# Attention by pairs of heads, run three chunks behind the query projection

## The chip, the cores and the metric

The kernel runs on one NeuronCore of a Trainium2 chip. A core has a tensor engine (PE, with its weight loads PEld), a vector engine (DVE), a scalar engine (ACT), GpSimd (POOL) and a sync engine (SP), which here issues the loads of weights. The metric is device time in microseconds (us), the median of three runs. The kernel before takes 1352.44 us (1351.33 to 1356.03).

## The reference

One inference step of a two-layer encoder with width 1024: layer 0 is RWKV-7 time mixing and a mixture of experts, layer 1 is window attention and a mixture of experts. There are 256 prompt frames and 64 sample frames, so 320 in all, in five chunks of 64. The change touches only the attention of layer 1:

```python
def sink_probs(s, sink, mask):
    ...
    m = jnp.maximum(jnp.max(s, axis=-1, keepdims=True), sink)
    e = jnp.exp(s - m)
    return e / (jnp.sum(e, axis=-1, keepdims=True) + jnp.exp(sink - m))

# 16 query heads, 4 key/value heads, head size 64; a chunk of 64 queries sees its own
# chunk of keys and the two before (the sample chunk: 128 cached keys and its own 64)
    q = (h @ p['at_w_q'][j] + p['at_b_q'][j]).reshape(B, S, N_HEADS, HEAD_DIM)
    q = rope_partial(q, pos)
    s = jnp.einsum('bnqkgd,bnskd->bnkgqs', qc, kb).astype(jnp.float32) * ATT_SCALE
    ...
    o = jnp.einsum('bnkgqs,bnskd->bnqkgd', probs.astype(vb.dtype), vb)
    return o @ p['at_w_o'][j] + p['at_b_o'][j]
```

## The kernel before

Activations lie transposed: 1024 features as eight blocks `c` of 128 partitions, 320 time columns each. A block of the queries `q[:, c, :]` holds two heads of 64 rows, called a pair below; pairs 2g and 2g+1 share key/value head g. All of it is in float32.

Each engine runs its own list of instructions in program order. A key such as `("prob", n, c)` stands for a count of finished instructions on one engine; `wait` on it holds everything behind it on the waiting engine. PSUM has eight banks, taken in turn by `Banks.open`, which waits until the bank's last reader is done.

After the experts of layer 0, PE makes the key and value projections, turns the values into rows of tokens (`v64`), and then makes the query projection: for every block c, eight matmuls of 128x320 (`project`), and, one block late, a matmul with the rotation matrix (`q_turn`). ACT adds the bias while it copies out of PSUM; DVE applies cosine and sine (three operations a block).

Then comes the attention proper, by time chunks n = 0 to 4, each over all 16 heads at once. `scores(n)` writes four banks of 16 heads x 64 queries x W keys, W being 64, 128, 192, 192, 192. DVE takes the row maxima and combines them with the sinks (`row_maxima`), ACT takes exponentials with row sums (`exps`, one instruction for a pair, then one for the sinks), DVE adds, inverts and scales (eight instructions). PE turns the probabilities in pieces of 64 keys (`attended`, line 1181), ACT copies these out of PSUM, and PE multiplies them with the values. On PE the order is: scores(0), scores(1), attended(0), scores(2), attended(1), and so on: the scores of chunk n+1 stand between those of chunk n and the turning of chunk n's probabilities. The output projection (`project("ao", ...)`) waits for the whole of it. SP loads the second half of its weights when the query projection has released the slot, and the first experts' weights of layer 1 behind it in the same queue.

Of the kernel before, what the change touches and what calls it, by code (L numbers as in the profile page):

```python
# [237 lines left out]
def build(nc, i, o, known, seen):  # L238
    ctx = ExitStack()
    with ctx:  # L240
# [22 lines left out]
        sink = sb("sink", [P, C])  # L263
        att2 = sb("att", [P, 2, 6, C])
# [98 lines left out]
        hkv, haq, q, qt, oT = E[1], E[5], E[6], E[7], E[5]  # L363
# [6 lines left out]
        v64 = work[0:64, 4 * B:4 * B + 7 * 256].rearrange("p (n d) -> p n d", n=7)  # L370
        k64 = work[0:64, 4 * B + 1792:4 * B + 2560].rearrange("p (n d) -> p n d", n=3)
        prob2 = [work[:, a:a + 1536].rearrange("p (c s) -> p c s", c=C) for a in (0, 7 * B)]
        pT = work[0:64, 1536:1536 + 3072].rearrange("p (w c s) -> p w c s", w=3, c=C)
# [212 lines left out]
        def _(eng):  # L586
# [65 lines left out]
            eng.dma_start(v64[:, 4:6, :], i["cache_v"][0].rearrange("(w t) n d -> t w (n d)", w=2)  # L652
# [5 lines left out]
            pl.wait("v64")  # L658
            for n_out, w, t0 in ((5, 2, 0), (5, 3, 64), (9, 6, 0)):
                put(o[n_out][0, t0:t0 + 64].rearrange("t n d -> t (n d)"), v64[:, w, :])  # L660
# [12 lines left out]
        def _(eng):  # L673
# [460 lines left out]
            for w, t0 in enumerate((0, 64, 128, 192, 256)):  # L1134
                pb = bank.open("v64", w)
                for c in range(2):
                    ins = eng.transpose(pb[0:64, P * c:P * c + P], vT[:, c, t0:t0 + 64], ident)
                full(ins, "v64", w)
# [11 lines left out]
            for c in range(C):  # L1150
                project("q", [c], haq, lambda hf: ("wq", hf), ("h", "A1"))
                if c:
                    q_turn(c - 1)
            q_turn(C - 1)
            pe.wait("kswapped", 1)

            def scores(n):
                t0 = CH * n
                lo, hi = (max(0, n - 2) * CH, (n + 1) * CH) if n < 4 else (256, 448)
                for b in range(4):  # L1160
                    pe.wait("q ready", 2 * b + 1)
                    pb = bank.open("score", n, b)
                    for cc in range(2):
                        c = 2 * b + cc
                        g = c // 2
# [5 lines left out]
                    full(ins, "score", n, b)  # L1171

            def attended(n):
                prob = prob2[n % 2]
                parts = min(n + 1, 3) if n < 4 else 3
                for w in range(parts):
                    for hf in range(2):
                        pe.wait("prob", n, 4 * hf + 3)
                        pb = bank.open("pT", n, w, hf)
                        for cc in range(4):  # L1180
                            ins = eng.transpose(pb[0:64, P * cc:P * cc + P], prob[:, 4 * hf + cc, CH * w:CH * w + CH],
                                                ident)
                        full(ins, "pT", n, w, hf)
                pe.wait("v64")
                pe.wait("pT ready", n)
                pb = bank.open("o", n)
                first = max(0, n - 2) if n < 4 else 4
                for g in range(NKV):
                    for h in range(2):
                        for w in range(parts):  # L1190
                            ins = mm(pb[64 * h:64 * h + 64, P * g:P * g + P].rearrange("p (c s) -> p c s", c=2),
                                     v64[:, first + w, 64 * g:64 * g + 64],
                                     pT[:, w, 2 * g:2 * g + 2, 64 * h:64 * h + 64], w == 0, w == parts - 1)
                full(ins, "o", n)

            scores(0)
            for n in range(NCH):
                if n + 1 < NCH:
                    scores(n + 1)  # L1200
                attended(n)
            pe.wait("oT", NCH - 1)
            project("ao", range(C), oT, lambda hf: ("ao", hf))
# [12 lines left out]
        def _(eng):  # L1216
# [130 lines left out]
            def moe(l):  # L1347
# [5 lines left out]
                eng.wait_ge(in_sems["out_written"], (64, 160)[l])  # L1353
# [68 lines left out]
            for w in range(5):  # L1422
                act(v64[:, w if w < 4 else 6, :], pk("v64", w)[0:64, 0:256], ACT.Copy, ("read", "v64", w), ("v64",))
            for w in range(3):
                act(k64[:, w, :], pk("k64", w)[0:64, 0:256], ACT.Copy, ("read", "k64", w), ("k64",))
            for c in range(C):
                act(q[:, c, :], pk("q", c)[:, 0:T], ACT.Identity, ("read", "q", c), ("qraw", c),
                    bias=vcol("at_b_q", c))

            def exps(n):  # L1430
                W = min(n + 1, 3) * CH if n < 4 else 192
# [11 lines left out]
            for n in range(NCH):  # L1443
                parts = min(n + 1, 3) if n < 4 else 3
                for w in range(3):
                    if w == 2 and n + 1 < NCH:
                        exps(n + 1)
# [16 lines left out]
        def _(eng):  # L1464
# [467 lines left out]
            for n in range(NCH):  # L1932
# [9 lines left out]
                if n + 1 < NCH:  # L1942
                    row_maxima(n + 1)
# [45 lines left out]
```

## Time and profile before

| | us |
|---|---|
| median of three runs | 1352.44 |
| the profiled execution | 1351.86 |
| its span, from the first to the last instruction | 1350.1 |
| PE busy, all of the span | 1144.0 (85%) |
| DVE busy | 525.3 (39%) |
| ACT busy | 343.2 (25%) |
| query projection, 870.7 to 909.9 | 39.2 |
| attention proper, 909.9 to 973.9 | 64.0 |

### The profile page before, as it was taken

To read this page: it belongs to the slowest core of one execution; us is meant where nothing else is said; L and a number is where in the kernel's file an instruction comes from. 1 tells how busy PE (TensorE), PEld (TensorE's weight loads), DVE (VectorE), ACT (ScalarE), POOL (GpSimd) and SP (SyncE) were. 2 spreads that over 40 slices of the span, in tenths; PEclk is the share of its full clock that TensorE was granted. 3 is DMA by queue.
4 is the path that set the end of the run, shared out by engine and by line. 5 is a ranking of instruction groups with operands and counts; after the bars stand their busy time and mean duration, and the time that the engine had idled before them with its cause. 6 is when DMAs were issued, how large, how long until landed. Compare 5 with 4: busy or idle time off the path is not lost.

```text
span 1350.1 us, 23468 instructions
## 1 busy us (share of the span) xinstructions
PE 1144.0 (85%) x9621; PEld 669.3 (50%) x9621; DVE 525.3 (39%) x1320; ACT 343.2 (25%) x652; POOL 61.4 (5%) x69
## 2 busy tenths in 40 slices
PE   5579998788878887789999995996894899999993
PEld 2146665566657654534444443665772544444442
DVE  3422194433231245424344335235137134344434
ACT  1122231111111303133333223115313233333312
POOL 2000000000000000000000001000000000001000
PEclk9689999999999988889999998997796999999997
DMA  9533116866763342049999967005031099999921
GB/s 249 162 125 125 66 60 232 305 228 245 251 252 127 102 192 112 1 200 421 422 425 428 426 288 257 12 12 238 1 124 63 0 377 422 427 426 426 423 112 39
DMA packets 45992, 297.19 MB, mean 220 GB/s; under 512 B 5972, under 2 KB 7352, under 8 KB 22360
## 3 DMA queue, kind: packets, MB, share of 16 engines
q1 hardware_dynamic: 43856, 290.17, 54.1%
q0 software_dynamic: 1856, 5.79, 1.9%
q8 instruction: 63, 1.03, 0.3%
q14 instruction: 17, 0.14, 0.0%
q10 hardware_dynamic: 200, 0.06, 0.0%
HBM read 293.77 MB, written 2.24 MB: 219 GB/s over the span
## 4 chain that ended last, share of the span: by engine, by line
PE 74%; DVE 11%; DMA 10%; ACT 2%; issue 2%; SPq 0%; ACTq 0%; DVEq 0%; POOL 0%; POOLq 0%
PE bank L679 72%; DMA ring<-in_ada_w 9%; DVE work L1475 3%; ACT work L1225 2%; DMA ring<-in_kv_ada_w 1%; DVE work L1481 1%; DVE work L1478 1%; DVE x_res L1481 1%; DVE rstd L1513 1%; DMA ring<-in_rw_w_rkv 1%; DVE work L1845 1%; PE bank L1056 1%; DVE work L1832 1%; DVE ring L1475 1%; DVE att L1923 1%
## 5 line engine op out<-in xcount | busy, mean ns | idle before, releaser
L679 PE MATMUL bank<-ring,work 128*64 128x512 f32 (+1 forms) x1760 | 351.3, 552 | 9.3 <-DVE work L1832 7.7
L679 PE MATMUL bank<-work,ring 128*128 128x320 f32 (+3 forms) x1600 | 297.9, 362 | 30.9 <-DVE work L1475 8.4
L679 PE MATMUL bank<-work 128*128 128x320 bf16 (+7 forms) x1842 | 237.1, 302 | 47.5 <-DVE work L1756 14.8
L679 PEld LDWEIGHTS bank<-work,ring 128*128 128x128 f32 (+2 forms) x1600 | 211.0, 169 | 118.8 <-issue 29.5
L679 PEld LDWEIGHTS bank<-work 128*128 128x128 bf16 (+2 forms) x1842 | 175.5, 130 | 117.5 <-issue 36.7
L679 PEld LDWEIGHTS bank<-ring,work 128*64 128x64 f32 (+1 forms) x1760 | 118.8, 138 | 218.4 <-issue 211.3
L1225 ACT ACTIVATE work<-bank 128x320 f32<-128x320 f32 (+6 forms) x116 | 58.7, 551 | 252.4 <-PE bank L679 227.7
L679 PE MATMUL bank<-ring 64*64 64x64 f32 (+2 forms) x2624 | 103.7, 233 | 1.9 <-issue 1.9
L679 PEld LDWEIGHTS bank<-ring 64*64 64x64 f32 (+2 forms) x2624 | 93.8, 143 | 22.1 <-issue 18.3
L679 PE MATMUL bank<-ring,cs 128*32 128x512 f32 x448 | 64.6, 657 | 38.0 <-DMA ring<-in_ada_w 32.0
L1826 DVE SCALAR_TENSOR_TENSOR work<-work,small,bank 128x256 f32<-128x256 f32 x32 | 21.5, 673 | 172.9 <-ACT work L1389 89.1
L1225 ACT ACTIVATE ring<-bank 128x512 f32<-128x512 f32 (+3 forms) x67 | 37.7, 563 | 197.1 <-PE bank L679 196.1
L1845 DVE TENSOR_TENSOR work<-work,bank 128x320 f32<-128x320 f32 x128 | 62.4, 488 | 37.4 <-PE bank L679 37.4
L1839 DVE TENSOR_TENSOR work<-bank,work 128x512 f32<-128x512 f32 x64 | 44.1, 689 | 61.9 <-ACT work L1393 61.9
L1475 DVE TENSOR_TENSOR ring<-ring,bank 128x512 f32<-128x512 f32 x45 | 29.1, 685 | 86.5 <-PE bank L679 86.5
L633 POOL TENSOR_TENSOR work<-work 128x512 bf16<-128x512 f32 x32 | 36.4, 1159 | 541.3 <-ACT work L1397 541.3
L1393 ACT ACTIVATE work<-bank 128x512 bf16<-128x512 f32 x64 | 38.0, 593 | 49.2 <-PE bank L679 49.2
L1481 DVE SCALAR_TENSOR_TENSOR work<-work,vec 128x320 f32<-128x320 f32 x56 | 27.0, 546 | 53.9 <-PE bank L679 53.5
L679 PE MATMUL bank<-work,const 128*128 128x320 f32 (+1 forms) x128 | 34.0, 486 | 13.2 <-ACT work L1225 6.9
L1377 ACT ACTIVATE work<-work 128x512 f32 x64 | 40.0, 633 | 14.1 <-issue 14.1
L679 PEld LDWEIGHTS bank<-ring,cs 128*32 128x32 f32 x448 | 10.4, 112 | 65.8 <-DMA ring<-in_ada_w 46.9
L1397 ACT ACTIVATE work<-work 128x512 bf16<-128x512 f32 x64 | 40.1, 626 | 8.6 <-DVE work L1839 8.6
(180 smaller groups left out, 753.4 us busy)
## 6 DMA issues: line engine op xcount, KB each, us to landing
ring<-in_moe_w_gu SPq DMA_DIRECT2D x64, 2048.0 KB, 13.9
ring<-in_moe_w_down SPq DMA_DIRECT2D x64, 1024.0 KB, 14.1
ring<-in_ada_w SPq DMA_DIRECT2D x40, 1024.0 KB, 5.1
ring<-in_rw_w_rkv SPq DMA_DIRECT2D x6, 2048.0 KB, 8.0
ring<-in_ada_w SPq DMA_DIRECT2D x4, 2048.0 KB, 28.8
ring<-in_kv_ada_w SPq DMA_DIRECT2D x8, 1024.0 KB, 5.0
ring<-in_rw_w_o SPq DMA_DIRECT2D x2, 2048.0 KB, 11.6
ring<-in_at_w_q SPq DMA_DIRECT2D x2, 2048.0 KB, 13.8
```

Of the source, the lines that this page charges most:

```text
L633: eng.tensor_tensor(dpart[:, 0, 2, cols], rest[:, n, :], dpart[:, 0, 1, cols], ALU.subtract).then_inc(S["lo_ready0"], 1)
L679: return eng.matmul(out, l, r, start=start, stop=stop, **kw)
L1056: ins = eng.transpose(ps[0][:, 2 * P * u + P * f:2 * P * u + P * f + P], hid[:, u, P * f:P * f + P], ident)
L1225: ac.did(eng.activation(out, in_, f, **kw), *keys)
L1377: eng.activation(xe[:, u, :, 64 * v:64 * v + 64], xall[:, :, bass.ds(at, SLOTS)], ACT.Copy).then_inc(S["xe_ready"], 1)
L1393: eng.activation(dpart[:, u, 0, 512 * n:512 * n + 512], ps[4 + n][:, :], ACT.Copy).then_inc(S["hi_ready"], 1)
L1397: eng.activation(dpart[:, u, 1, 512 * n:512 * n + 512], rest[:, n, :], ACT.Copy).then_inc(S["mid_ready"], 1)
L1475: op(eng.tensor_tensor(out, a, b, o_), *keys)
L1481: op(eng.scalar_tensor_tensor(out, a, s_, b, o1, o2), *keys)
L1826: eng.scalar_tensor_tensor(hid_w[:, u], silu[:, u, :].rearrange("p (q f) -> p q f", f=2), wslot[:, u:u + 1], ps[3 + 4 * u][:, FE:2 * FE].r ...
L1839: eng.tensor_tensor(rest[:, n, :], ps[4 + n][:, :], dpart[:, u, 0, 512 * n:512 * n + 512], ALU.subtract).then_inc(S["rest_ready"], 1)
L1845: eng.tensor_tensor(ysum[:, c, :], ysum[:, c, :], ps[(6, 1, 2)[c % 3]][:, 0:T], A_).then_inc(S["y_added"], 1)
```

## The change

The attention is cut the other way. A step now covers one pair of heads c = 0 to 7 over all five chunks of time (`SPAN` gives, for each chunk, its keys, its bank and its column there). The pieces are strung between the query projections: in step s, PE does the turning of pair s-3, the query projection s, the weighted values of pair s-3, the rotation of s-1 and the scores of pair s-2. DVE and ACT follow in the same order. Probabilities are turned in pieces of 128 keys and of 64 keys (`PAIR`, `LONE`) and multiplied with value tiles of 128 or 64 tokens (`VTILES`, some of them overlapping): eight transposes and 16 matmuls of 64 columns a pair. The separate add for the sinks is gone (its operand is the bias of the exponential), and the output projection waits block by block. The value rows for the output are now two DMAs instead of three. The waits for `kswapped` and for the value tiles stand ahead of the query projection.

```diff
+SPAN = [(0, 64, 0, 0), (0, 128, 0, 64), (0, 192, 1, 0), (64, 256, 1, 192), (256, 448, 0, 192)]
+PCOL = [0, 64, 384, 576, 192]
+VTILES = [(0, 128), (64, 128), (128, 128), (192, 64), None, (256, 64)]
+PAIR = [None, (0, 0), (0, 1), (1, 2), (4, 3)]
+LONE = [(0, 0), None, (2, 1), (3, 2), (5, 3)]
...
+            def scores(c):
+
+                g = c // 2
+                pe.wait("q ready", c)
+                for b in range(2):
+                    pb = bank.open("score", c, b)
+                    for n, (lo, hi, at, col) in enumerate(SPAN):
+                        if at != b:
+                            continue
                         for h in range(2):
                             var = 0 if g % 2 == h else 2
                             r = slice(64 * h, 64 * h + 64)
-                            ins = mm(pb[r, 256 * cc:256 * cc + hi - lo], q[r, c, t0:t0 + CH],
+                            ins = mm(pb[r, col:col + hi - lo], q[r, c, CH * n:CH * n + CH],
                                      kT[r, var + g // 2, lo:hi], True, True)
...
+            def prob_turn(c):
+
+                pe.wait("prob", c)
+                prob = prob2[c % 2]
+                pb = bank.open("pT", c, 0)
+                for n in range(1, NCH):
+                    ins = eng.transpose(pb[:, P * (n - 1):P * n], prob[:, PCOL[n]:PCOL[n] + P], ident)
+                full(ins, "pT", c, 0)
+                pb = bank.open("pT", c, 1)
+                for k, n in enumerate((0, 2, 3, 4)):
+                    a = PCOL[n] + (P if n else 0)
+                    ins = eng.transpose(pb[0:64, P * k:P * k + P], prob[:, a:a + 64], ident)
+                full(ins, "pT", c, 1)
+
+            def attended(c):
+
+                g = c // 2
+                pe.wait("pT ready", c)
+                pT = pT2[c % 2]
+                pb = bank.open("o", c)
+                for n in range(NCH):
                     for h in range(2):
...
+                        terms = []
+                        if PAIR[n]:
+                            terms.append((P, PAIR[n], 0))
+                        if LONE[n]:
+                            terms.append((64, LONE[n], 1))
+                        for m, (k, (tile, at), w) in enumerate(terms):
+                            ins = mm(pb[64 * h:64 * h + 64, CH * n:CH * n + CH],
+                                     vtok[0:k, tile, 64 * g:64 * g + 64], pT[0:k, w, at, 64 * h:64 * h + 64],
+                                     m == 0, m == len(terms) - 1)
+                full(ins, "o", c)
+
+            pe.wait("kswapped", 1)
+            pe.wait("vtok")
+            for s in range(C + 3):
+                if s == C:
+                    q_turn(C - 1)
+                if s >= 3:
+                    prob_turn(s - 3)
+                if s < C:
+                    project("q", [s], haq, lambda hf: ("wq", hf), ("h", "A1"))
+                if s == C:
+                    scores(C - 2)
+                if s >= 3:
+                    attended(s - 3)
+                if 1 <= s < C:
+                    q_turn(s - 1)
+                if 2 <= s < C:
+                    scores(s - 2)
+                if s == C:
+                    scores(C - 1)
+            project("ao", range(C), oT, lambda hf: ("ao", hf), ("oT",))
...
+            def row_maxima(c):
+
+                att = att2[:, c % 2]
+                a, b = [pk("score", c, k) for k in range(2)]
+                for n, w, col in ((0, 64, 0), (1, 128, 64), (4, 192, 192)):
+                    op(eng.tensor_reduce(att[:, 0, n:n + 1], a[:, col:col + w], AX.X, ALU.max))
+                op(eng.tensor_reduce(att[:, 0, 2:4], b[:, 0:384].rearrange("p (n s) -> p n s", n=2), AX.X, ALU.max))
+                ve.settle()
+                ts(att[:, 1, 0:NCH], att[:, 0, 0:NCH], -SCALE, nsink[:, c:c + 1], M, ALU.min, ("row max", c))
...
+            for s in range(1, C + 1):
+                rotated(s - 1)
+                if s >= 2:
+                    row_maxima(s - 2)
+                    normalized(s - 2)
+            row_maxima(C - 1)
+            normalized(C - 1)
```

The first rows are PE's in the kernel before, where the attention begins: the last rotation matmul (`const_phase`), the scores of chunks 0 and 1, and then the turning of chunk 0 (L1181).

```order
L679 MATMUL bank<-work,const_phase 128x320 [waits act_done]
L679 MATMUL bank<-work 64x64 [waits dve_done]
L679 MATMUL bank<-work 64x64 x3
...
L679 MATMUL bank<-work 64x128 x16
L1181 MATMUL bank<-const,work 64x128 [waits act_done,dve_done]
L1181 MATMUL bank<-const,work 64x128 x3
```

Between the 64-column scores of chunk 0 and the transposes that use them stand the 16 score matmuls of chunk 1. The next rows are PE's in the changed kernel, from the end of step 3 to the end of step 4: rotation, scores of pair 1 (64x64, 64x128, 64x192), turning of pair 1 (L1184, L1189), projection 4 (`ring`), values of pair 1, rotation 3.

```order
L688 MATMUL bank<-work,const_phase 128x320
L688 MATMUL bank<-work 64x64 x2
L688 MATMUL bank<-work 64x128 x2
L688 MATMUL bank<-work 64x192 x6
L1184 MATMUL bank<-const,work 128x128 [waits dve_done]
L1184 MATMUL bank<-const,work 128x128 x3
L1189 MATMUL bank<-const,work 64x128 x4
L688 MATMUL bank<-work,ring 128x320 [waits ring_in2]
L688 MATMUL bank<-work,ring 128x320 x7
L688 MATMUL bank<-work 64x64 [waits act_done]
L688 MATMUL bank<-work 64x64 x15
```

The transposes that wait for DVE stand right behind the ten score matmuls of the same pair; the projection has moved behind them. The next rows are DVE's in the changed kernel for one step: the rotation of one block (three rows), then the maxima (L1956, L1957), the wait for ACT and the scaling of one pair.

```order
L1505 TENSOR_TENSOR work<-const_phase,bank 128x320 [waits pe_done]
L1505 TENSOR_TENSOR work<-work,const_phase 128x320
L1505 TENSOR_TENSOR work<-work 128x320 [waits dve_done]
L1956 TENSOR_REDUCE att<-bank 128x1 [waits pe_done]
L1956 TENSOR_REDUCE att<-bank 128x1 x2
L1957 TENSOR_REDUCE att<-bank 128x2
L1508 TENSOR_SCALAR att<-att,nsink 128x5 [waits dve_done]
L1505 TENSOR_TENSOR att<-att 128x5 [waits act_done]
L1967 RECIPROCAL att<-att 128x5 [waits dve_done]
L1508 TENSOR_SCALAR work<-work,att 128x64 [waits dve_done]
L1508 TENSOR_SCALAR work<-work,att 128x128
L1508 TENSOR_SCALAR work<-work,att 128x192 x3
```

Before, the three rotation rows stood eight times in a block of their own, ahead of all maxima; the scaling then had eight rows of one width. The last rows are ACT's in the changed kernel: the table load, the exponentials of pair 0, the copies of its turned probabilities, the bias of projection 3, and the copy of the output of pair 0.

```order
L1252 ACT_TABLE_LOAD
L1252 ACTIVATE work,att<-bank,att 128x64 [waits dve_done]
L1252 ACTIVATE work,att<-bank,att 128x128
L1252 ACTIVATE work,att<-bank,att 128x192 x3
L1252 ACTIVATE att<-att,sink 128x5
L1252 ACTIVATE work<-bank 128x512 [waits pe_done]
L1252 ACTIVATE work<-bank 64x512 [waits pe_done]
L1252 ACTIVATE work<-bank,vec 128x320 [waits pe_done]
L1252 ACTIVATE work<-bank 128x320 [waits pe_done]
```

This table load is the only one between the query projection and the next norm, as before; the bias instructions now stand among the exponentials.

## Rows read from the trace of the kernel before

**Rows 1.** The page: busy us (share of the span) and instructions.
```profile
PE 1144.0 (85%) x9621; PEld 669.3 (50%) x9621; DVE 525.3 (39%) x1320; ACT 343.2 (25%) x652; POOL 61.4 (5%) x69
```
**Rows 2.** Windows: stretch, its us, busy us by engine, PE clock, DMA share, GB/s.
```profile
870.70:909.90 39.20, 39.12 (x148) 27.09 (x146) 9.09 (x20) 6.14 (x14) 3.17 (x6) 1.00 0.05 11
909.90:973.90 64.00, 46.98 (x449) 39.76 (x448) 23.05 (x90) 31.54 (x115) 0.00 (x0) 0.76 0.33 132
```
**Rows 3.** Timeline of PE: start, us, engine, line, operation, count, idle before.
```profile
870.67 8.78 PE L679 MATMUL bank<-work,ring 128*128 128x320 f32 x32
...
879.83 4.47 PE L679 MATMUL bank<-work,ring 128*128 128x320 f32 x16
...
909.87 0.92 PE L679 MATMUL bank<-work 64*64 64x64 f32 x24
911.89 2.20 PE L679 MATMUL bank<-work 64*64 64x64 f32 x40 [1.10 <-DVE work L1475]
917.86 1.91 PE L1181 MATMUL bank<-const,work 128*64 128x128 f32 x8 [3.77 <-DVE work L1478]
920.45 6.90 PE L679 MATMUL bank<-work 64*64 64x128 f32 x48 [0.68 <-ACT work L1225]
927.29 1.94 PE L1181 MATMUL bank<-const,work 128*64 128x128 f32 x16
931.16 4.53 PE L679 MATMUL bank<-work 64*64 64x128 f32 x64 [1.94 <-ACT work L1225]
...
970.12 3.11 PE L679 MATMUL bank<-work 64*64 64x128 f32 x48 [0.77 <-ACT work L1225]
```
**Rows 4.** Timeline of DVE in the attention: maxima and scaling by width.
```profile
912.49 0.89 DVE L1923 TENSOR_REDUCE att<-bank 128x2 f32<-128x128 f32 x4 [0.65 <-PE bank L679]
918.37 1.41 DVE L1923 TENSOR_REDUCE att<-bank 128x2 f32<-128x256 f32 x4
927.51 1.95 DVE L1923 TENSOR_REDUCE att<-bank 128x2 f32<-128x384 f32 x4 [1.96 <-PE bank L679]
929.69 0.17 DVE L1478 TENSOR_SCALAR att<-att 128x8 f32<-128x8 f32 x1
933.56 0.17 DVE L1475 TENSOR_TENSOR att<-att 128x8 f32<-128x8 f32 x1 [3.49 <-ACT att L1225]
933.76 0.20 DVE L1938 RECIPROCAL att<-att 128x8 f32<-128x8 f32 x1
934.00 1.93 DVE L1478 TENSOR_SCALAR work<-work,att 128x192 f32<-128x192 f32 x8
```
**Rows 5.** The chain that ended last, in order of time: ACT's part.
```profile
914.01 2.48 ACT work L1225 x16
...
930.10 3.33 ACT work L1225 x16
933.43 0.11 ACT att L1225
```
**Rows 6.** Windows, columns as in Rows 2: granted clock in the attention.
```profile
914.00:917.80 3.80, 0.09 (x2) 0.00 (x0) 1.11 (x7) 2.57 (x17) 0.00 (x0) 0.87 1.10 433
...
920.40:927.30 6.90, 6.85 (x49) 5.51 (x49) 2.03 (x10) 3.49 (x19) 0.00 (x0) 0.52 1.04 440
```
**Rows 7.** Timeline of PE: dense float32 bursts, two of them after an idle stretch.
```profile
829.38 7.27 PE L679 MATMUL bank<-work,const 128*128 128x320 f32 x16 [6.30 <-DVE coef L1478]
843.68 19.86 PE L679 MATMUL bank<-work,ring 128*128 128x320 f32 x64 [7.04 <-DVE work L1478]
...
1008.47 4.47 PE L679 MATMUL bank<-work,const 128*128 128x320 f32 x16
```
**Rows 8.** Timeline of ACT: a copy of turned probabilities.
```profile
918.96 0.59 ACT L1225 ACTIVATE work<-bank 64x512 f32<-64x512 f32 x1 [2.37 <-PE bank L1181]
```
**Rows 9.** Timeline of SP: the first load for the experts of layer 1.
```profile
908.96 0.58 SPq L492 DMA_DIRECT2D ring<-in_moe_w_gu  x1
```
**Rows 10.** DMA issues: KB each, us to landing.
```profile
ring<-in_at_w_o SPq DMA_DIRECT2D x2, 2048.0 KB, 14.0
```

More of the change, by code:

```diff
@@ L1148, in q_turn @@
                 full(mm(pb[:, 0:T], acst("ropep"), q[:, c, :], True, True), "qrot", c)
[L1150 to L1165, printed above, removed]
+            def scores(c):
[5 more added lines that the diff above has]
+                        if at != b:
+                            continue
                         for h in range(2):
@@ L1197, in _ @@
[L1197 to L1203, printed above, removed]
+                    full(ins, "score", c, b)
+            def prob_turn(c):
[10 more added lines that the diff above has]
+                full(ins, "pT", c, 1)
@@ L1421, in _ @@
                 act(kT[:, 2 + c, :], pk("kswap", c)[:, 0:448], ACT.Copy, ("read", "kswap", c), ("kswapped", c))
-            for w in range(5):
-                act(v64[:, w if w < 4 else 6, :], pk("v64", w)[0:64, 0:256], ACT.Copy, ("read", "v64", w), ("v64",))
+            for w, tile in enumerate(VTILES):
+                if tile is not None:
+                    act(vtok[0:tile[1], w, :], pk("vtok", w)[0:tile[1], 0:256], ACT.Copy, ("read", "vtok", w),
+                        ("vtok",))
             for w in range(3):
@@ L1425, in _ @@
                 act(k64[:, w, :], pk("k64", w)[0:64, 0:256], ACT.Copy, ("read", "k64", w), ("k64",))
[L1426 to L1431, printed above, removed]
-                prob, att = prob2[n % 2], att2[:, n % 2]
-                for b in range(4):
-                    ac.wait("row max", n, b)
-                    for cc in range(2):
-                        c = 2 * b + cc
-                        act(prob[:, c, 0:W], ps[seen_bank(("score", n, b))][:, 256 * cc:256 * cc + W], ACT.Exp,
-                            ("read", "score", n, b), ("exp", n, c), bias=att[:, 1, c:c + 1], scale=SCALE,
-                            accum_out=att[:, 2, c:c + 1])
-                act(att[:, 3, :], att[:, 4, :], ACT.Exp, ("sink exp", n))
@@ L1442, in _, with exps @@
-            exps(0)
[L1443 to L1447, printed above, removed]
-                    for hf in range(2 if w < parts else 0):
-                        act(pT[:, w, 4 * hf:4 * hf + 4, :],
-                            pk("pT", n, w, hf)[0:64, :].rearrange("p (c s) -> p c s", c=4), ACT.Copy,
-                            ("read", "pT", n, w, hf), ("pT ready", n))
-                act(oT[:, :, CH * n:CH * (n + 1)], pk("o", n)[:, :].rearrange("p (c t) -> p c t", c=C), ACT.Copy,
-                    ("read", "o", n), ("oT", n))
+            def exps(c):
+                prob, att = prob2[c % 2], att2[:, c % 2]
+                ac.wait("row max", c)
+                for n, (lo, hi, b, col) in enumerate(SPAN):
+                    act(prob[:, PCOL[n]:PCOL[n] + hi - lo], ps[seen_bank(("score", c, b))][:, col:col + hi - lo],
+                        ACT.Exp, ("read", "score", c, b), ("exp", c), bias=att[:, 1, n:n + 1], scale=SCALE,
+                        accum_out=att[:, 2, n:n + 1])
+                act(att[:, 3, 0:NCH], att[:, 1, 0:NCH], ACT.Exp, ("sink exp", c), bias=sink[:, c:c + 1])
@@ L1913, in _ @@
                 ve.settle()
[L1914 to L1925 removed]
+                tt_(q[:, c, :], q[:, c, :], qrot2[c % 2], A_, ("q ready", c))
@@ L1926, in row_maxima, with normalized @@
+            def normalized(c):
+                prob, att = prob2[c % 2], att2[:, c % 2]
+                ve.wait("sink exp", c)
+                tt_(att[:, 5, 0:NCH], att[:, 2, 0:NCH], att[:, 3, 0:NCH], A_)
                 ve.settle()
-                ts(att[:, 1, :], att[:, 1, :], -1.0, None, M, ALU.bypass)
+                op(eng.reciprocal(att[:, 5, 0:NCH], att[:, 5, 0:NCH]))
                 ve.settle()
-                tt_(att[:, 4, :], sink[:, :], att[:, 1, :], A_, *[("row max", n, b) for b in range(4)])
```

104 lines of the change are left out of this document (44 added, 60 removed).

## The prediction

> **What bounds the kernel now.** The page first [rows 1]: PE is busy for 85% of the span, DVE and ACT for 39 and 25%. So PE's list is the one to follow, and the change must be read as what it does to PE. Next the windows by stage [rows 2]. In the query projection PE works 39.12 of 39.2 us at the full clock, with DVE at 9 us and ACT at 6. In the attention proper it works 46.98 of 64.0 us at a mean clock of 0.76. That is the stretch the change takes apart, and the obvious hope is that the projection, in which DVE and ACT have little to do, can cover the attention's waits. The timeline of PE [rows 3] then shows what the 64.0 us are made of: runs of score, transpose and value matmuls with 1.94 to 3.77 us of waiting for the softmax in between; the timeline of DVE and the chain that ended last [rows 4, 5] show the softmax itself, DVE and ACT in turn. Last, two windows [rows 6]: after the wait of 3.77 us the granted clock is 0.52 for the 6.9 us from 920.4 on, so the same matmuls take twice as long. After the wait of 1.94 us at 931.16 [rows 3] they run at full speed again (compare the transposes: 8 in 1.91 us at 917.86, 16 in 1.94 us at 927.29).
>
> From the first projection matmul (870.67) to the first one of the output projection (973.9) it is 103.2 us. Everything the change touches lies in there. I forecast the same stretch of the changed kernel.
>
> **PE's work for one pair, at the full clock.** A projection: from 870.67 to 879.83 stand two projections and one rotation matmul, 36 - 2 = 34 records of 0.269 us, so a projection (16 records) is 4.31 and a rotation matmul (2 records) 0.54 us [rows 3]. Scores: chunks 0 and 1 took 0.92 + 2.20 = 3.12 us. The burst at 931.16 is the values of chunk 1 (32 records) and the scores of chunk 3. The value row at 970.12, 48 records in 3.11 us, gives 65 ns a record, so 2.1 for 32, and 4.53 - 2.1 = 2.4 us for scores 192 wide. All five chunks are 3.12 + 3 x 2.4 = 10.4 us; the new order has the same 80 matmuls of the same widths, so 1.3 us a pair. Turning: 96 transposes of 0.121 us (1.94/16) become 64. Four of a pair's eight are 128 columns wide in the loaded operand and not 64, but all stream 128 columns, so 8 x 0.121 = 0.97 us. Values: 96 matmuls of 128 columns become 128 of 64, 32 records a pair. No row has them with 128 partitions: the lower bound is 49 ns a record (3.12 us for the 64 records of scores), 1.6 us; the value row's 65 ns gives 2.1; if the records with 128 partitions shared the array with nothing, twice that, 4.2. I take 1.8, between the two near rows. Together 4.31 + 0.54 + 1.3 + 0.97 + 1.8 = 8.9 us a step; all eight pairs are 71 us, where before 39.2 + 12.5 (values) + 10.4 + 11.6 (turning) = 73.7. By work alone the change gives little.
>
> The value matmuls now alternate between tiles of 128 and of 64 rows, some 13 changes a pair, where before all were 64 by 64. The Trainium skill (TensorEngine Tiling (Array Packing), Key Properties) says that changing the tiling mode, unlike changing the tile, drains the engine. No row before alternates like this, and the page gives no price; if a change cost one record of the value row, it would be 0.8 us a pair and some 7 us on the sum.
>
> **The wait in each step.** The order of the changed kernel decides the case. In step s, scores of pair s-2 are PE's last work, and the first of step s+1 is the turning of the same pair, which needs its whole softmax. The projection, which could cover it, stands behind the waiting transposes, and so does everything else on PE. So the softmax is laid bare six times (after steps 2 to 7). Its length, from the last score matmul: DVE is still about 0.1 us in the rotation of the next block. Maxima of 64, 128, 192 and 384 columns: the rows give 0.22, 0.35 and 0.49 us for 128, 256 and 384 [rows 4], so 0.16 + 0.22 + 0.29 + 0.49 = 1.2; one small operation, 0.2. ACT: an exponential with its sum takes 0.31 us at 64 columns (2.48/8) and 0.42 at 192 (3.33/8) [rows 5], so 0.31 + 0.36 + 3 x 0.42 = 1.9, and the sink's 0.1 with its hand-over, 2.1 in all. DVE: add and reciprocal 0.4, then the scaling, 0.24 for 192 columns (1.93/8) [rows 4], five in 1.1. With hand-overs of 0.04 us, 5.2 us. The two small operations that the change saves are in this already. Six waits: 31.2 us. In the order before, 16 score matmuls of the next chunk stood between, and one softmax served 16 heads: five chains of 8 exponentials against now eight of 5.
>
> **The clock.** The idle stretches of 3.77, 6.30 and 7.04 us were each followed by matmuls at 1.2 GHz [rows 3, 6, 7]; one of 1.94 us was not. A wait of 5.2 us is well inside the first kind. What a cold start costs when a dense float32 burst follows is in two rows [rows 7]: 7.27 us at 829.38 where the same 16 records took 4.47 at 1008.47, so 2.8 lost; 19.86 us at 843.68 for 64 records that cost 4 x 4.31 = 17.2, so 2.6 lost. Here the burst is 1 us of transposes, then a projection: 2.7 us a step, for steps 3 to 7, 13.5 us. Bounds: nothing, if the clock held, and 4.6 a step, half of the 9.2 us at half speed from 917.86 to 927.1.
>
> **The end.** With step 8 the projections are gone. The path at the full clock: turning of pair 5 (1.0), scores of 6 (1.3), softmax of 6 (5.2), then in ACT's list the exponentials of 7 stand ahead of the copies for 6: maxima of 7 (1.4), ACT (2.1), two copies of 0.6 [rows 8], values of 6 (1.8), turning of 7 (1.0), the last copy (0.6), values of 7 (1.8): 17.4 us. PE's 6.9 us of it double at half speed: 24.3. PE is thinly used here, so I take 24 for this path and what a low clock still costs at the start of the output projection. That projection itself starts without the old wait of 0.7 us, as only its eighth block needs the last pair.
>
> **What is hidden.** The bias and copy instructions of ACT and the rotations of DVE lie beside PE's work: in a step ACT has about 5 us and DVE 5. The moved wait for the value tiles is put at 0.2 us, since ACT's copies end with PE's last transposes there. SP issues the second half of the output weights when the last projection is done, now late, at about 966, and the experts' loads of layer 1 behind it, which began at 908.96 [rows 9]. The half is needed four output blocks after the start (about 1017); landing took 14.0 us [rows 10]: hidden. If that cover were gone, it would be late by what exceeds some 50 us. POOL has one DMA less. Each costs nothing.
>
> **The sum.** 0.2 for the tiles; steps 0 to 2: 3 x 4.31 + 2 x 0.54 + 1.3 = 15.3; six waits 31.2; five steps' work 44.7 (unrounded 8.93 each); clock 13.5; the end 24. Together 128.9 us against 103.2: +25.7. On the profiled execution's own 1351.86 us this is 1377.6; that execution lies 0.6 below the median of the runs, so 1378 us.
>
> **The rivals.**
> - The clock holds: waits as above, no cold starts, the end at 17.4. 0.2 + 15.3 + 31.2 + 44.7 + 17.4 = 108.8, +5.6: 1358 us. For it: each burst is 8.9 us of dense work, more than before between waits. Against it: no idle stretch of over 3.7 us in the rows left the clock up.
> - The clock is low for most of a burst: 4.6 a step and 27 at the end (24.3 and 2.7): 141.4, +38: 1391 us. For it: the bursts of 64 by 64 matmuls stayed low for 9 us [rows 6]. Against: dense bursts did not [rows 7].
> - The other side, the softmax of one pair hides: if PE waited only 2 us a step, the clock would stay up as it did after 1.94 us, and 0.2 + 15.3 + 12 + 44.7 + 17.4 = 89.6, -13.6: 1339 us. With the clock up, faster begins at waits under (103.2 - 77.6)/6 = 4.3 us, but 3.77 already lowered it; with cold starts and the long end, waits would have to be 0.9. So it decides at about 3 us. The chain of five exponentials alone is 1.9, and DVE's share before and after it 2.7, so I see no way to 3.
> - The change does not do what it says, the waits being placed elsewhere: the order printed for the changed kernel shows them, so I give it nothing. A reload of the activation table between bias and exponential would be a like case; the order has one load.
>
> **How the numbers follow.** Chances: forecast 0.65, low clock throughout 0.15, clock holds 0.14, softmax hides 0.03, an unseen gain or cover that ends near no change 0.03. The likeliest case's own range is 1370 to 1385 (values at 1.6 or 2.1 and at the drain's 0.8 more, the softmax 0.3 either way six times, the end between 20 and 26). The range of 8 in 10 reaches up to the second case and down to near the third: 1360 to 1391. What a measurement here can tell from no change is 0.3%, 4 us: faster 0.03, same 0.05 (0.03 and a tail of the case at 1358), slower 0.92.
>
> **What would show it.** In the profile after: six idle stretches of PE before L1184, each 5 to 5.5 us and released by DVE's scaling; the granted clock at 0.5 at the start of each following burst and at 1.0 at its end; a step of about 16.8 us; value matmuls of 1.6 to 2.1 us a pair at full clock; the stretch to the first output projection of about 129 us; and nothing changed behind it. I am wrong if PE's idle time before the transposes is under 3 us, if the clock stays at 1.0 through the steps, or if the time differs outside this stretch.

## The result, and the profile after

The changed kernel takes 1402.45 us (median of four runs, 1401.01 to 1405.5); the kernel before, with a fourth run beside it, 1354.24 us. The ratio is 1.0347, with an interval of 1.0323 to 1.0372: slower by 3.5%, some 48 us where the prediction had 26, and outside its range of 1360 to 1391.

The page of the changed kernel, first the span and then the line of busy times (busy us, share of the span, instructions):

```profile
span 1399.2 us, 23531 instructions
```
```profile
PE 1172.5 (84%) x9653; PEld 681.3 (49%) x9653; DVE 527.2 (38%) x1332; ACT 341.5 (24%) x650; POOL 60.7 (4%) x68
```

Against [rows 1] PE is busy for 28.5 us more, in a change that was to take a little work off it; DVE and ACT are as before. So the span of 49.1 us more is waiting and also busier matmuls. The windows of the changed kernel, cut where the first three steps end and where the sixth wait begins (stretch, its us, busy us by engine, clock, DMA share, GB/s):

```profile
874.20:889.90 15.70, 15.68 (x72) 10.88 (x72) 2.72 (x6) 3.65 (x7) 2.72 (x5) 1.00 0.10 26
889.90:987.40 97.50, 70.66 (x393) 48.44 (x391) 21.34 (x76) 21.48 (x75) 0.00 (x0) 0.79 0.05 16
987.40:1021.10 33.70, 24.36 (x162) 17.67 (x162) 9.93 (x39) 10.52 (x41) 0.00 (x0) 0.66 0.49 204
```

From the first matmul of the query projection to the first of the output projection it is 146.9 us, where [rows 2] add up to 103.2: 43.7 of the 49.1 us are in this stretch. Another 2.3 are in the output projection behind it, which starts at the low clock, and 3.5 lie ahead of it, where the stretch now begins (874.2 for 870.7). The program ahead differs only in the value tiles and the wait for them (0.23 us of idle time); in the profiles of the experiments below this start lies anywhere from 869.1 to 881.7, so nearly all of it is scatter.

PE's timeline in the changed kernel, from the third step to the fifth, with three later rows of scores (start, us, engine, line, operation, records, idle before), and its last row:

```profile
888.42 1.53 PE L688 MATMUL bank<-work 64*64 64x64 f32 x20
895.32 1.11 PE L1184 MATMUL bank<-const,work 128*128 128x128 f32 x4 [5.37 <-DVE work L1508]
896.23 1.06 PE L1189 MATMUL bank<-const,work 128*64 128x128 f32 x4
897.08 5.67 PE L688 MATMUL bank<-work,ring 128*128 128x320 f32 x16
902.67 3.53 PE L688 MATMUL bank<-work 64*64 64x64 f32 x32
906.13 1.30 PE L688 MATMUL bank<-work,const_phase 128*128 128x320 f32 x2
907.36 2.66 PE L688 MATMUL bank<-work 64*64 64x64 f32 x20
915.39 1.11 PE L1184 MATMUL bank<-const,work 128*128 128x128 f32 x4 [5.37 <-DVE work L1508]
...
927.43 2.83 PE L688 MATMUL bank<-work 64*64 64x64 f32 x20
...
947.66 2.83 PE L688 MATMUL bank<-work 64*64 64x64 f32 x20
...
967.85 1.53 PE L688 MATMUL bank<-work 64*64 64x64 f32 x20
...
1015.66 5.54 PE L688 MATMUL bank<-work 64*64 64x64 f32 x32 [0.68 <-ACT work L1252]
1021.12 37.01 PE L688 MATMUL bank<-work,ring 128*128 128x320 f32 x128
```

Each step ends with scores (888.42, 907.36) and then PE stands for 5.37 us until DVE has scaled the same pair. That was forecast as 5.2. The row at 902.67 is the surprise: the 32 records of value matmuls of one pair take 3.53 us. (A merged row bears the shape of its first matmul: of these 16 matmuls, eight are 128 rows deep.) The windows around it in the changed kernel show at which clock:

```profile
895.30:899.50 4.20, 4.18 (x13) 3.22 (x14) 0.00 (x0) 1.19 (x2) 0.00 (x0) 0.50 0.00 0
899.50:906.30 6.80, 6.80 (x45) 4.70 (x45) 0.00 (x0) 0.59 (x2) 0.00 (x0) 1.00 0.00 0
906.30:909.70 3.40, 3.40 (x22) 2.06 (x22) 1.38 (x3) 0.38 (x1) 0.00 (x0) 0.50 0.00 0
```

The value matmuls ran at the full clock, so a record costs 110 ns, where [rows 3] had 65 at twice the columns. And after them the clock fell, at 906.3, although PE had been busy for every one of the 6.80 us before: the low stretch after the wait was expected, this second one, in steps 3 to 5 (scores in 2.66 to 2.83 us, against 1.53 in step 6), was not. The softmax behind the 5.37 us, on DVE, against [rows 4]:

```profile
910.14 0.69 DVE L1956 TENSOR_REDUCE att<-bank 128x1 f32<-128x64 f32 x3 [1.26 <-PE bank L688]
910.75 0.55 DVE L1957 TENSOR_REDUCE att<-bank 128x2 f32<-128x384 f32 x1
911.33 0.23 DVE L1508 TENSOR_SCALAR att<-att,nsink 128x5 f32<-128x5 f32 x1
913.77 0.17 DVE L1505 TENSOR_TENSOR att<-att 128x5 f32<-128x5 f32 x1 [2.21 <-ACT att L1252]
...
914.20 1.14 DVE L1508 TENSOR_SCALAR work<-work,att 128x64 f32<-128x64 f32 x5
```

Maxima 1.2, ACT 2.2, scaling 1.14: each term as taken, and 0.1 more of small operations and hand-overs.

### The profile page after: what moved, and what is told of

Read it like the earlier page. It is cut to its first block, busy times and chain, and to the rows that moved or that the text cites. A ratio compares the mean times of both kernels' runs of the same rounds, so it can differ in the third digit from the quotient of the medians.

```text
span 1399.2 us, 23531 instructions
## 1 busy us (share of the span) xinstructions
PE 1172.5 (84%) x9653; PEld 681.3 (49%) x9653; DVE 527.2 (38%) x1332; ACT 341.5 (24%) x650; POOL 60.7 (4%) x68
## 4 chain that ended last, share of the span: by engine, by line
PE 74%; DVE 11%; DMA 10%; ACT 3%; issue 2%; SPq 0%; ACTq 0%; DVEq 0%; POOL 0%; POOLq 0%
PE bank L688 72%; DMA ring<-in_ada_w 8%; DVE work L1505 3%; ACT work L1252 2%; DVE work L1508 1%; DMA ring<-in_kv_ada_w 1%; DVE work L1511 1%; DVE x_res L1511 1%; DVE rstd L1543 1%; DMA ring<-in_rw_w_rkv 1%; PE bank L1184 1%; DVE work L1875 1%; PE bank L1065 1%; DVE work L1862 0%; DVE ring L1505 0%
## 5 line engine op out<-in xcount | busy, mean ns | idle before, releaser
L688 PE MATMUL bank<-work,ring 128*128 128x320 f32 (+3 forms) x1600 | 309.1, 373 | 31.4 <-DVE work L1505 8.9
L688 PE MATMUL bank<-work 128*128 128x320 bf16 (+7 forms) x1906 | 250.9, 292 | 43.0 <-DVE work L1786 14.9
L688 PEld LDWEIGHTS bank<-work,ring 128*128 128x128 f32 (+2 forms) x1600 | 218.5, 176 | 122.9 <-issue 36.5
L688 PEld LDWEIGHTS bank<-work 128*128 128x128 bf16 (+3 forms) x1906 | 181.2, 129 | 123.9 <-issue 41.8
L1252 ACT ACTIVATE work<-bank 128x320 f32<-128x320 f32 (+6 forms) x111 | 55.5, 539 | 272.3 <-PE bank L688 242.5
L688 PEld LDWEIGHTS bank<-ring,cs 128*32 128x32 f32 x448 | 10.6, 111 | 66.8 <-DMA ring<-in_ada_w 45.6
## 6 DMA issues: line engine op xcount, KB each, us to landing
ring<-in_ada_w SPq DMA_DIRECT2D x4, 2048.0 KB, 28.4
```

What stands on the lines that cost most here:

```text
L688: return eng.matmul(out, l, r, start=start, stop=stop, **kw)
L1252: ac.did(eng.activation(out, in_, f, **kw), *keys)
```

## The experiments

Theory A, formed on this profile: there are two losses. One is the softmax laid bare by the order, 5.4 us a step, with the cold starts that follow (bursts that begin at the low clock). The other is the change of tile shape between value matmuls of 128 and of 64 rows. The list of instructions has 12 such changes a pair; the prediction and the expectations below counted 13. The times of the runs in one table; the stretch goes from the first matmul of the query projection to the first of the output projection in the profiled execution. "Before" is the median of the kernel before on the same chip.

| run | us | before | ratio (95%) | stretch, us | values, us a pair at full clock |
|---|---|---|---|---|---|
| changed kernel | 1402.45 | 1354.24 | 1.0347 (1.0323 to 1.0372) | 146.9 | 3.53 |
| few | 1381.47 | 1358.95 | 1.0160 (1.0099 to 1.0221) | 127.8 | 1.59 |
| padded | 1383.81 | 1358.95 | 1.0196 (1.0139 to 1.0253) | 125.7 | 1.20 |
| side | 1382.54, one run | 1355.44 | - | 129.7 | 2.03 |
| pieces64 | 1384.39 | 1356.29 | 1.0198 (1.0151 to 1.0244) | 130.2 | 1.78 |
| fill | 1390.20 | 1358.95 | 1.0252 (1.0199 to 1.0304) | 132.6 | 3.53 |
| fill_padded | 1360.11 | 1355.44 | 1.0043 (1.0020 to 1.0067) | 109.4 | 1.20 |
| order | 1355.47 | 1358.95 | 0.9979 (0.9954 to 1.0004) | 101.0 | 3.5 (with the scores) |
| order_padded | 1336.26 | 1355.44 | 0.9842 (0.9798 to 0.9885) | 82.2 | 1.2 (with the scores) |
| best | 1336.30 | 1355.44 | 0.9863 (0.9831 to 0.9895) | 81.1 | 1.2 (with the scores) |

Where the scores stand ahead of the values in one row, the value in the last column is the row less 1.3 to 1.5 for the scores.

### Few changes of shape

```diff
-                for n in range(NCH):
-                    for h in range(2):
...
+                for n, kinds in ((0, "l"), (2, "lp"), (1, "p"), (3, "pl"), (4, "lp")):
+                    for m, kind in enumerate(kinds):
+                        k, (tile, at), w = (P, PAIR[n], 0) if kind == "p" else (64, LONE[n], 1)
+                        for h in range(2):
```

> The changed kernel with the value matmuls of a pair in another order: both heads side by side, and all matmuls of one tile shape together, so that the shape changes 3 times a pair instead of 13. Theory A, the change of shape is what costs (3.53 us a pair at full clock in the changed kernel, about 0.15 us from the last record of one shape to the first of the next): values fall to about 1.6 us a pair, the extra stretch at 1.2 GHz inside a step goes, and the time falls by 16 to 22 us, to 1380 to 1387. Theory B, a matmul with 128 rows and 64 columns shares the array with nothing: its 16 records still cost 0.11 us each, values stay at 2.3 us or more, and the time falls by less than 12 us.

Values took 1.59 us a pair, and the clock fell once a step and not twice. PE's timeline of the run named few:

```profile
910.20 1.59 PE L688 MATMUL bank<-work 64*64 64x64 f32 x32
911.72 0.81 PE L688 MATMUL bank<-work,const_phase 128*128 128x320 f32 x2
912.45 1.53 PE L688 MATMUL bank<-work 64*64 64x64 f32 x20
919.35 1.12 PE L1184 MATMUL bank<-const,work 128*128 128x128 f32 x4 [5.37 <-DVE work L1504]
```

The same 16 matmuls with the same operands, in another order, cost less than half, and the rotation and scores behind them run at the full clock (0.81 and 1.53 us; 1.30 and 2.66 in the changed kernel). The stretch is 19.1 us shorter. The runs of this kernel spread from 1373.6 to 1389.7, so its ratio is loose; the profile is what decides. Theory A holds; B, that 128 rows cost by themselves, would have left 2.3 us.

### All value matmuls 128 rows deep

```diff
-                            terms.append((64, LONE[n], 1))
+                            terms.append((P, LONE[n], 1))
...
+            for b in range(2):
+                op(eng.memset(pT2[b][64:128, 1], 0.0))
+            for w in (3, 5):
+                op(eng.memset(vtok[64:128, w, :], 0.0), ("padded",))
```

> The changed kernel with every value matmul 128 rows deep: the lone pieces of 64 keys are read with 64 rows of zeros below them (set once), in the old order. There is one tile shape in the value matmuls, 128 by 64, and no change. Theory A (changes of shape cost): 1.6 to 2.1 us a pair, time 1380 to 1388. Theory B (128 rows cost by themselves): 32 records of 0.11 us, 3.5 us a pair as in the changed kernel, time 1398 to 1405.

1.20 us a pair, 37 ns a record: half the array's rows multiply zeros in half of the matmuls, and it is three times as fast. PE's timeline of the run named padded:

```profile
906.26 1.20 PE L688 MATMUL bank<-work 128*64 128x64 f32 x32
...
915.03 1.12 PE L1184 MATMUL bank<-const,work 128*128 128x128 f32 x4 [5.37 <-DVE work L1509]
```

The order of heads is that of the changed kernel, so the order of heads does not cost anything where no shape changes. Rival B, 3.5 us, is out. The time, 1383.8, is within what A gave; the values, at 1.20 us, came out below its 1.6 to 2.1.

### The heads side by side, six changes

```diff
+                for n, kinds in ((0, "l"), (1, "p"), (2, "pl"), (3, "pl"), (4, "pl")):
```

> The changed kernel with both heads side by side in the value matmuls but the chunks in their own order, so 6 changes of shape a pair where the changed kernel has 13 and the run named few 3. If each change costs the same (0.39 us for 3 of them between few and padded, 0.13 each): 1.2 + 6 x 0.13 = 2.0 us a pair at full clock. If the old order's 3.53 us came from the heads standing one behind the other: 1.6 us as in few.

The loops are those of few, only the order of the list differs. 2.03 us in each pair. With 0, 3, 6 changes the price is 1.20, 1.59, 2.03: 0.13 to 0.15 us a change. Twelve changes give 2.8 to 3.0 by that; the changed kernel has 3.53. The rest, 0.5 to 0.8 us, may be that a change between every two matmuls also keeps the two heads, which use different column halves, from running together. No run shows that by itself.

### Pieces of 64 keys: half of the change alone

The part of the edit that turns the probabilities:

```diff
+PIECES = [(n, w) for n in range(5) for w in range(min(n + 1, 3))]
...
+                for b in range(3):
+                    pb = bank.open("pT", c, b)
+                    for k in range(4):
+                        n, w = PIECES[4 * b + k]
+                        a = PCOL[n] + 64 * w
+                        ins = eng.transpose(pb[0:64, P * k:P * k + P], prob[:, a:a + 64], ident)
```

> Half of the change alone: pairs of heads and the order of steps as in the changed kernel, but probabilities turned in pieces of 64 keys as in the kernel before (12 transposes a pair, 24 value matmuls of 64 rows, all of one tile shape, three copies by ACT). Theory A (changes of shape cost; the turning in 128 and 64 is what brought them): values 1.8 to 2.4 us a pair at full clock in place of 3.53 although there are 24 matmuls in place of 16, turning 1.45 in place of 0.97, one low stretch a step in place of two, time 1383 to 1392, 10 to 19 us under the changed kernel. Rival, the loss lies in the number and size of the value matmuls (64 columns each, too short to pay for their weight loads): 24 of them cost more than 16, values at 4 us or more, and the time is 1405 or above.

Timeline of PE in the run named pieces64:

```profile
906.97 1.78 PE L690 MATMUL bank<-work 64*64 64x64 f32 x48
...
916.31 2.77 PE L1186 MATMUL bank<-const,work 128*64 128x128 f32 x12 [5.36 <-DVE work L1499]
```

24 matmuls of one shape cost 1.78 us, 37 ns a record as in padded; 16 of two shapes cost 3.53. So the pairs of heads in the small pieces of the kernel before would have been 1384 us: of the changed kernel's loss of some 48 us, the pieces of 128 and 64 made about 20 (the ratios 1.0347 and 1.0198 differ by 0.015) and the order the rest.

### The waits filled

These lines stand behind the scores in steps 2 to 7:

```diff
+                    pb = bank.open("fill", s)
+                    for m in range(9):
+                        ins = mm(pb[:, 0:T], acst("swap"), haq[:, m % C, :], True, True)
+                    pe.did(ins, ("fill", s), ("read", "fill", s))
```

> The changed kernel with nine matmuls of 128x320 that nobody uses put behind the scores in steps 2 to 7, so that PE works through most of each wait for the softmax (4.8 of 5.4 us). The waits keep their length; only the clock can move. Theory A, the low clock after each wait costs some 3.5 us a step: the clock stays at 1.0 through the steps, and the time falls by 14 to 20 us, to 1382 to 1388. Rival: the clock falls because of the value matmuls and not because of the wait, so that it falls here too and the time stays within 5 us of 1402.

The ratio went from 1.0347 to 1.0252, 13 us: less than the 14 to 20 of theory A, and more than the 5 of its rival. PE's timeline of the run named fill shows why:

```profile
896.44 0.66 PE L1184 MATMUL bank<-const,work 128*128 128x128 f32 x4 [0.33 <-DVE work L1512]
...
912.86 0.66 PE L1184 MATMUL bank<-const,work 128*128 128x128 f32 x4 [0.33 <-DVE work L1512]
...
934.62 3.53 PE L688 MATMUL bank<-work 64*64 64x64 f32 x32
938.08 1.36 PE L688 MATMUL bank<-work,const_phase 128*128 128x320 f32 x2
939.36 2.60 PE L688 MATMUL bank<-work 64*64 64x64 f32 x20
...
947.33 0.66 PE L1184 MATMUL bank<-const,work 128*128 128x128 f32 x4 [0.33 <-DVE work L1512]
```

The turnings behind the filled waits now run at the full clock (0.66 us, not 1.11), and the step from 896.44 to 912.86 takes 16.42 us, where the first in the changed kernel took 20.07. But behind the value matmuls the clock fell here too. Two windows of fill:

```profile
934.60:938.10 3.50, 3.50 (x34) 2.61 (x33) 0.00 (x0) 0.53 (x1) 0.00 (x0) 1.00 0.00 0
938.20:941.60 3.40, 3.40 (x20) 2.17 (x22) 1.38 (x3) 0.42 (x1) 0.00 (x0) 0.50 0.00 0
```

So each theory was half right: the wait lowers the clock, and the alternating value matmuls can lower it without a long wait, here in two of the five steps.

### The waits filled, with one shape

> The run named padded with nine unused matmuls of 128x320 behind the scores in steps 2 to 7. Here neither waits nor changes of shape can lower the clock in the steps, and the waits keep their length, so the difference to padded is the price of the cold starts alone. Theory A: 2.9 us a step (a step of 16.8 us in padded against 5.4 + 8.5 of wait and work), five steps and part of the end, 14 to 19 us under padded, ratio to the kernel before about 1.006. Rival, the clock costs what the prediction took, nothing more: 13.5 us.

This is the edit of fill on padded. All five steps ran at the full clock, 14.09 us each (turnings begin at 890.86 and 904.95) against 16.1 to 17.0 in padded: 2.0 to 2.9 us for a cold start, where the prediction had 2.7, and 13.0 in five steps, where it had 13.5. So the rival's price of a cold start fits better than the 2.9 of theory A; the rest of the gain lies behind these steps. The stretch fell from 125.7 to 109.4 us, and the output projection behind it from 35.5 to 34.6, so 17 us together, inside what A gave. The ratios, 1.0196 and 1.0043, would be 21 us; with their intervals this is no contradiction, but the start scatter mentioned above is in them and not in the 17.

### Another order

```diff
             for s in range(C + 3):
...
+                if s < C:
+                    project("q", [s], haq, lambda hf: ("wq", hf), ("h", "A1"))
+                if 1 <= s <= C:
+                    q_turn(s - 1)
+                if s >= 3:
+                    prob_turn(s - 3)
+                if 2 <= s <= C:
+                    scores(s - 2)
+                if s >= 3:
+                    attended(s - 3)
+                if s == C:
+                    scores(C - 1)
```

> The changed kernel with another order in a step: projection, rotation, turning of pair s-3, scores of pair s-2, values of pair s-3 (ACT's list follows). All instructions are the same; the softmax of a pair now has the values, the projection and the rotation of the next step over it. Theory A, the six waits of 5.4 us and the cold starts behind them are the larger part of the loss: waits under 0.5 us in steps 3 to 7, the time falls by 45 to 52 us, to 1350 to 1358, about the time of the kernel before. Rival, the value matmuls lower the clock by themselves: the time falls by the waits alone, 27 to 33 us, to 1370 to 1375.

0.9979, the interval just reaching 1: the whole loss is gone, with the same instructions. Waits of PE in its stretch (who waited for whom, total us, times, longest), of the changed kernel, then of order:

```profile
PE bank L1184 <- DVE work L1508: 32.1, 7, 5.4
PE bank L688 <- ACT work L1252: 4.3, 3, 3.4
```
```profile
PE bank L688 <- ACT work L1248: 4.3, 3, 3.4
PE bank L1184 <- DVE work L1502: 2.8, 3, 1.3
```

29.3 us of waiting less, and 45.9 us less in the stretch: the difference, 16.6 us, is time at the low clock, as PE has the same matmuls. The rival, a loss of the waits alone, is out, though its premise is seen here too. These are windows of order in which PE never idled, and the clock fell behind the values of a pair all the same, in one of the five steps:

```profile
923.30:928.00 4.70, 4.70 (x53) 3.70 (x53) 1.89 (x7) 2.34 (x11) 0.00 (x0) 1.00 0.00 0
928.00:931.80 3.80, 3.80 (x9) 2.46 (x9) 1.50 (x7) 0.76 (x4) 0.00 (x0) 0.56 0.00 0
```

### Both repairs

> Both repairs in one: the order of the run named order (projection, rotation, turning, scores, values) and value matmuls all 128 rows deep as in the run named padded. Theory A (two separate losses: the softmax laid bare together with the cold starts, and the changes of tile shape): the gains add up, values 1.2 us a pair, no stretch at 1.2 GHz in the steps, 16 to 22 us under the run named order, ratio to the kernel before 0.980 to 0.986. Rival, one bound that both repairs touch (PE would find another wait once the values are short, above all the softmax, which the values partly cover): waits of 1 to 2 us come back in each step and the gain is under 12 us, ratio above 0.989.

The two add up: 0.9842, 1336.26 us. PE's timeline of one step in order_padded:

```profile
902.66 4.57 PE L688 MATMUL bank<-work,ring 128*128 128x320 f32 x16
907.07 0.70 PE L688 MATMUL bank<-work,const_phase 128*128 128x320 f32 x2
907.61 0.60 PE L1184 MATMUL bank<-const,work 128*128 128x128 f32 x4
908.05 0.60 PE L1189 MATMUL bank<-const,work 128*64 128x128 f32 x4
908.58 2.66 PE L688 MATMUL bank<-work 64*64 64x64 f32 x52
911.16 4.58 PE L688 MATMUL bank<-work,ring 128*128 128x320 f32 x16
```

8.5 us a step (902.66 to 911.16) with no wait and no low clock, where the changed kernel has 20.07 (895.32 to 915.39). The rival's waits do not come back: projection, rotation and values, 6 us, cover the 5.4 of the softmax.

### Another end

Against order_padded:

```diff
                 if 2 <= s <= C:
                     scores(s - 2)
+                if s == C:
+                    scores(C - 1)
                 if s >= 3:
                     attended(s - 3)
-                if s == C:
-                    scores(C - 1)
```

with ACT in the same order, and DVE taking the maxima of pair 7 before it scales pair 6.

> The run named order_padded with another end: the scores of pair 7 stand right behind those of pair 6, ahead of the values of pair 5, and DVE takes the maxima of 7 before it scales 6, so that ACT goes from the exponentials of 6 straight to those of 7. Theory A: the wait of 3.36 us for the copies of pair 6 behind the exponentials of 7 goes, and the end shortens by 3 to 6 us; ratio to the kernel before 0.975 to 0.983. Rival: the wait only moves to the turning of pair 6, nothing measurable.

Missed: 1336.30 us against 1336.26, nothing measurable. PE's timeline at the end of the run named best:

```profile
936.92 1.11 PE L1184 MATMUL bank<-const,work 128*128 128x128 f32 x4 [3.50 <-DVE work L1503]
...
946.34 0.66 PE L1184 MATMUL bank<-const,work 128*128 128x128 f32 x4 [2.94 <-DVE work L1503]
...
948.44 2.03 PE L688 MATMUL bank<-work 128*64 128x64 f32 x32 [0.68 <-ACT work L1249]
...
955.01 35.79 PE L688 MATMUL bank<-work,ring 128*128 128x320 f32 x128
```

The wait for ACT's copies fell from 3.02 to 0.68 us as meant, and the one before the turning of pair 6 hardly grew (2.94 us, 2.78 in order_padded), so the rival's time came without its cause. But the last matmuls then ran at the low clock throughout, and so did the start of the output projection, 35.79 us where order_padded had 34.72. The 1.1 us won in the stretch (82.2 to 81.1) went there.

## Why the prediction was wrong

Its direction, its place and the mechanism that it named were right; one term of its sum was far too small, and behind it stood a second mechanism. By its own steps, against the profile after:

- **The wait.** Forecast 5.2 us six times, 31.2; measured 5.37 five times and once 5.3, partly filled by a rotation matmul, 32.2. The list of instructions, with durations of the rows, gave this to 0.2 us. Off by +1.0.
- **The first steps.** 15.3 forecast, 15.7 measured. +0.4.
- **Work of steps 3 to 7 and their clock.** Forecast 44.7 + 13.5 = 58.2; measured 70.6 (from 895.32 to 987.4, less four waits of 5.37). +12.4. This is the step that failed, and in it one term: the values, "I take 1.8, between the two near rows". They are 3.46 to 3.53, which is 8.5 us for five pairs at the full clock. Rotation and scores, 0.73 and 1.53 us for 0.54 and 1.3, add 2.1. The clock cost 15.3 us by the rows. Of these, 10.6 lie behind the waits (from the turning to the values 7.35, 7.56, 7.68, 7.80 and 6.90 us, 5.33 in fill), less than the 13.5 taken. The other 4.7 are the second low stretch in steps 3 to 5, behind the same value matmuls; few, with the same waits, has it in no step. So the clock's term came out near by two misses that partly cancel.
- **The end.** 24 forecast, 28.4 measured. +4.4, of which the values of pairs 6 and 7 are 3.9: 5.54 us each at the low clock, where 1.8 doubled is 3.6. The term was to hold the low clock at the start of the output projection too; with these 2.3 us the miss is 6.7.

In the stretch the misses are 18.2 us, where 128.9 was forecast and 146.9 measured; the 0.2 us between 18.2 and the difference are the wait for the value tiles, which fell just ahead of it. Take all or most of the changes of shape out and the forecast holds: 127.8 us in few, 125.7 in padded, 129.7 in side. So the mechanism that was forecast is worth what was forecast, and a second one was priced far too low.

The prediction had looked at this second one. It had the upper bound of 4.2 us for values, which held, and took a value next to the low end because the near rows lay there; but those rows were all of one shape, and the thing to be priced was the alternation. It cited the Trainium skill (TensorEngine Tiling (Array Packing), Key Properties: changing the tiling mode, unlike the tile, drains the engine), and then left it out of the sum, with a guess of one record, 0.065 us, a change. The runs agree that a change costs time, whether by a drain or not: 0.13 to 0.15 us each for three and six changes, and 3.53 against 1.20 us for a pair with twelve, 0.19 each. In the range, this uncertainty stood with 0.8 us a pair where 1.7 was needed, and the upper end of 1391 held no case with dear values.

**The rivals.** That the clock holds is refuted by each step of the profile after. That it is low for most of a burst came partly true (3.7 us lost in the first step, 20.07 against the 16.42 of fill, next to the 4.6 taken), but 1.6 of them for the reason just given. That the softmax hides was excluded rightly; it is what the order run makes true, with a stretch of 101.0 us, and with the values repaired 82.2, where that rival had 89.6. **Nothing behind the stretch** changed but the low clock in the output projection, as said. SP issued the second half of the output weights late, and no matmul of the output projection waited for it:

```profile
981.75 0.37 SPq L494 DMA_DIRECT2D ring<-in_at_w_o  x1
```

One reading in the prediction is imprecise. It takes the transposes at 927.29 as a sign that the wait of 1.94 us left the clock up, but they stand before that wait; the row that shows it is the burst at 931.16 itself [rows 3], 64 records in 4.53 us.

## What to carry to other kernels

Look in the list of the engine that bounds for a result that is asked for right behind the work that starts it: overlapping two stages gains only if the filler stands between the two, and the length of the bare chain can be added up from rows to a few per cent (here 5.2 against 5.37 us). Matmuls of different tile shapes should be grouped, or made one shape with zeros, before their count or their columns are reduced: here 16 alternating ones cost twice as much as 24 of one shape. When a row of the trace lacks the very property that is new (here the alternation), it is no middle value for it, and the range must reach to the bound.

## What was not expected of the hardware

- A change between 128-row and 64-row matmuls of 64 columns costs 0.13 to 0.15 us at 2.4 GHz (1.20, 1.59, 2.03 us for 0, 3, 6 changes), and more where nearly every matmul brings one (3.53 us for 12).
- The clock fell to 1.2 GHz behind 3.5 us of such alternating matmuls with PE busy throughout (at 928.0 in order, 938.2 in fill, 906.3 in the changed kernel), but not each time: in one, two and three of the five steps. Behind the values of the five steps of few, side, padded and pieces64 it never fell.
- Matmuls of 128 rows and 64 columns cost the same as those of 64 by 64: 37 ns a record in both (1.20 us for 32, 1.78 for 48). By the 0.269 us of a projection's record of 320 columns, one of 64 columns alone would be 54 ns (an estimate), so in both shapes neighbours seem to overlap in part.
